# A transformer step on one core: the first two features between the modulation blocks, sums on GpSimd, and one context tile for four heads

## The reference

```python
mod = silu(c) @ w_mod + b_mod                       # 9 vectors of 1024
h = rmsnorm(x, ng[0]) * (1 + sc1) + sh1
x = x + g1 * 0.5 * (silu(h @ w_gate) * (h @ w_up)) @ w_down      # first FFN, 2816 features
h = rmsnorm(x, ng[1]) * (1 + sc2) + sh2
q, k, v, xr, xg = split(h @ w_in)
# latent tokens attend to latent keys and 128 cached ones, context tokens to context keys only
s = einsum(q, k) / 8                                # 4 heads, two maps each
p = softmax(s)
o = (p[map 0] - lam * p[map 1]) @ v                 # then rmsnorm of each head
# beside it: convolution, gates and a scan over time of xr, times gelu(xg)
x = x + g2 * concat(o, rg) @ w_out
x = x + g3 * 0.5 * swiglu(rmsnorm(x) ...)           # second FFN
```

## Time and profile before

| | us |
|---|---|
| median of 3 runs | 2238.14 |
| lowest, highest | 2234.83, 2238.75 |
| the profiled execution's own time | 2237.18 |
| its span | 2235.4 |
| mean granted TensorE clock | 0.993 |

### The profile page before, as it was taken

One profiled execution on the slowest core, in us unless ns is written; L12 is line 12 of the kernel. 1 busy time (PEld: TensorE's weight loads), 2 busy tenths in 40 slices (PEclk: granted clock), 3 DMA queues, 4 the chain that ended last, 5 costly groups with the idle time before them and its releaser, 6 DMA issues.

```text
span 2235.4 us, 34069 instructions
## 1 busy us (share of the span) xinstructions
PE 2161.9 (97%) x13144; PEld 2100.3 (94%) x13144; DVE 1537.1 (69%) x2543; ACT 825.0 (37%) x1503; POOL 67.6 (3%) x120
## 2 busy tenths in 40 slices
PE   5999999999999999999999999999999999999997
PEld 4989999999999999899988889899999999999996
DVE  6977777777878865766767874695555547756556
ACT  5632232234212133565257762453222323411122
POOL 0000000000000000000023130000000000000000
PEclk9999999999999999999999999999999999999999
DMA  7333323334534403001133211132121223521312
GB/s 294 134 106 121 120 96 136 105 123 141 179 127 157 145 19 150 30 29 48 38 84 110 55 41 38 61 112 89 59 84 63 75 72 113 179 94 59 114 31 85
DMA packets 86133, 219.03 MB, mean 98 GB/s; under 512 B 10624, under 2 KB 38144, under 8 KB 86016
## 3 DMA queue, kind: packets, MB, share of 16 engines
q1 hardware_dynamic: 82176, 208.52, 27.4%
q0 software_dynamic: 3840, 8.92, 1.8%
HBM read 172.56 MB, written 35.92 MB: 93 GB/s over the span
## 4 chain that ended last, share of the span: by engine, by line
PE 87%; DVE 6%; ACT 3%; DMA 2%; issue 1%; SPq 0%; DVEq 0%; POOL 0%; ACTq 0%
PE ps L818 15%; PE ps L819 15%; PE ps L820 15%; PE ps L893 9%; PE ps L895 9%; PE ps L894 9%; PE ps L1073 7%; PE ps L1204 2%; PE ps L1149 1%; PE ps L1055 1%; PE ps L1190 1%; PE ps L1157 1%; DMA sb_stage<-in_w_mod 1%; ACT sb_pr L1721 1%; DVE sb_nmx L2461 1%
## 5 line engine op out<-in xcount | busy, mean ns | idle before, releaser
L818 PE MATMUL ps<-sb_hH,sb_wH 128*128 128x384 f32 x1664 | 563.0, 338 | 9.5 <-DVE sb_hL L1915 4.7
L819 PE MATMUL ps<-sb_hL,sb_wH 128*128 128x384 f32 x1664 | 557.2, 335 | 0.0
L820 PE MATMUL ps<-sb_hH,sb_wL 128*128 128x384 f32 x1664 | 557.2, 335 | 0.0
L818 PEld LDWEIGHTS ps<-sb_hH,sb_wH 128*128 128x128 f32 x1664 | 313.1, 188 | 16.9 <-DVE sb_hL L1915 5.4
L819 PEld LDWEIGHTS ps<-sb_hL,sb_wH 128*128 128x128 f32 x1664 | 313.4, 188 | 1.2 <-issue 0.3
L820 PEld LDWEIGHTS ps<-sb_hH,sb_wL 128*128 128x128 f32 x1664 | 313.3, 188 | 0.0
L2225 DVE SCALAR_TENSOR_TENSOR sb_x<-ps,sb_mod,sb_x 128x384 f32<-128x384 f32 (+2 forms) x384 | 186.1, 514 | 172.2 <-PE ps L820 167.0
L893 PE MATMUL ps<-sb_hH,sb_wH 128*128 128x384 f32 x704 | 236.2, 336 | 5.1 <-DVE sb_tmp L2085 3.9
L894 PE MATMUL ps<-sb_hL,sb_wH 128*128 128x384 f32 x704 | 235.9, 335 | 0.0
L895 PE MATMUL ps<-sb_hH,sb_wL 128*128 128x384 f32 x704 | 235.7, 335 | 0.0
L1368 ACT ACTIVATE sb_wH<-sb_wide 128x512 fp32r<-128x512 f32 x176 | 110.9, 633 | 228.7 <-DVE sb_wide L1969 223.7
(11 more groups left out here) (259 smaller groups left out, 3799.7 us busy)
## 6 DMA issues: line engine op xcount, KB each, us to landing
sb_raw<-in_w_gate SPq DMA_DIRECT2D x56, 512.0 KB, 3.6
sb_raw<-in_w_up SPq DMA_DIRECT2D x56, 512.0 KB, 3.5
sb_raw<-in_w_mod SPq DMA_DIRECT2D x56, 512.0 KB, 3.6
hidden<-sb_tmp SPq DMA_DIRECT2D x132, 192.0 KB, 2.1
sb_hid_raw<-hidden SPq DMA_DIRECT2D x40, 576.0 KB, 6.4
sb_raw<-in_w_dn SPq DMA_DIRECT2D x80, 256.0 KB, 2.6
sb_stage<-in_w_mod SPq DMA_DIRECT2D x4, 2048.0 KB, 15.7
sb_raw<-in_w_in SPq DMA_DIRECT2D x16, 512.0 KB, 3.5
```

The lines of the kernel that those rows point to most:

```text
L818: pe.matmul(o, wH, xH, start=begin, stop=False)
L819: pe.matmul(o, wH, xL, start=False, stop=False)
L820: return pe.matmul(o, wL, xH, start=False, stop=end)
```

## The change

**Head.** The seven small tensors that nothing early needs are loaded behind the first two modulation blocks. The weights of feature 0 are loaded ahead of the third and fourth block, those of features 1 and 2 and chunks 1 and 2 of x behind them. PE computes the k-steps 0 to 3 of feature 0 between the modulation blocks, and afterwards parts of features 0 and 1 in turn (`early_part`), as k-tiles of h come. ScalarE's casts and VectorE's lows follow that order, one 128x512 half at a time (`early_one`). The series of the recurrence moves into the down projection (`series_step`). PE's modulation blocks use bank 2 in place of 6, and feature 2 the banks 2 and 7.

**GpSimd.** The seven additions of the squares of chunk 2 (`last_square`) and the four differences of each of the four pairs (`op_differences`, in both FFNs) move from VectorE to GpSimd.

**Attention.** The four context tiles become one: eight score matmuls in the value projection (behind piece 8), one maximum per map over four heads, eight exponentials, four differences, four transposes, one copy, four value matmuls. The loop runs over 32 latent tiles. `SPLIT_AT` is moved accordingly.

The diff, cut:

```diff
-TILES = NH * QT
-KEY_TILES = [1] + [9] * 8
-GROUP0 = [0] + [1 + 3 * t for t in range(9)]
-GROUPS = GROUP0[9]
+LT = LAT // P
+TILES = 1 + NH * LT
+KEY_TILES = LT + 1
+LAST_HEAD = 1 + (NH - 1) * LT
...
-SPLIT_AT = {4: (1, 1), 8: (2, 0), 10: (2, 1), 17: (3, 0), 20: (3, 1)}
+SPLIT_AT = {4: (1, 1), 7: (2, 0), 9: (2, 1), 14: (3, 0), 17: (3, 1)}
...
+        def early_bank(z, w, u):
+            return (2, 7)[u] if (z, w) == (0, 2) else 3 + u + 2 * (w % 2)
...
                 for w in range(EARLY - 1):
-                    load_one(z, 0, w + 2, (MAIN + w + 2) % FT)
-                    load_one(z, 1, w + 2, (MAIN + w + 2) % FT)
+                    if z:
+                        early_load(z, w + 2)
                     store(z, 0, 0, MAIN + w, w)
+                    if z == 0 and w + 4 <= EARLY:
+                        early_load(z, w + 4)
...
+            for b in MOD_FIRST[:2]:
+                stage_load(b)
+            for dst, name in LATER_SMALLS:
+                sp.dma_start(dst, a[name]).then_inc(gw_in, 16)
+            early_load(0, 0)
+            for b in MOD_FIRST[2:]:
+                stage_load(b)
+            early_load(0, 1)
+            early_load(0, 2)
             x_load(1)
-            load_one(0, 0, 1, MAIN + 1)
-            load_one(0, 1, 1, MAIN + 1)
             x_load(2)
+            early_load(0, 3)
             ffn_loads(0)
...
+            def last_square(k):
+                s, buf = nrm[0], sum_buf(0, 2)
+                n = square_at(0, 2, k)
+                pool.wait_ge(s["sq"], n + 1)
+                if k > 1:
+                    pool.wait_ge(s["acc"], added_at(0, 2, k - 1))
+                pool.tensor_tensor(buf, buf if k > 1 else tmp[:, (n - 1) % 2], tmp[:, n % 2], ALU.add).then_inc(s["acc"], 1)
+            def op_differences(z, p):
+                base = 16 * z + 4 * p
+                pool.wait_ge(front, base + 4)
+                pool.tensor_tensor(op_raw(T1, p), op_raw(T3, p), op_raw(B11, p), ALU.subtract).then_inc(front_pool, 1)
+                pool.tensor_tensor(op_raw(T3, p), op_raw(B22, p), op_raw(T3, p), ALU.subtract).then_inc(front_pool, 1)
+                pool.wait_ge(front_pool, base + 1)
+                pool.tensor_tensor(op_raw(T2, p), op_raw(B22, p), op_raw(T1, p), ALU.subtract).then_inc(front_pool, 1)
+                pool.wait_ge(front_pool, base + 3)
+                pool.tensor_tensor(op_raw(T4, p), op_raw(B21, p), op_raw(T2, p), ALU.subtract).then_inc(front_pool, 1)
+            for k in range(1, KT):
+                last_square(k)
+            for p in range(KT // 2):
+                op_differences(0, p)
...
+                op_differences(1, p)
...
             mod_products(0)
             spread(0, 0)
-            for n in range(1, PRE):
-                mod_products(n)
-            def first_chunk(z, u, n, w, between=None, index=0):
...
+                             {(2, 0, 2): (stats, 1), (2, 1, 0): (spread, 1), (2, 1, 5): (stats, 2), (3, 0, 3): (spread, 2)})
...
+            def early_part(n, u, ks):
+                first_chunk(0, u, n + 1, None, lambda k: pe.wait_ge(nrm[0]["h"], k + 1), n, ks)
+            early_part(0, 0, (0, 1))
+            mod_products(2)
+            early_part(0, 1, (0, 1))
+            for u in range(2):
+                early_part(0, u, (2, 3))
+            mod_products(3)
+            early_part(1, 0, range(4))
+            for k in (4, 5):
+                for u in range(2):
+                    early_part(0, u, (k,))
+            early_part(1, 1, range(4))
+            for k in (6, 7):
+                for u in range(2):
+                    early_part(0, u, (k,))
+            for u in range(2):
+                early_part(1, u, range(4, KT))
             ffn_pe(0)
...
+            def context_scores():
+                for hd in range(NH):
+                    for m in range(2):
+                        r = slice(m * DH, (m + 1) * DH)
+                        mm = pe.matmul(ps[:, 6 + m, hd * P:(hd + 1) * P], x[r, hd, 0:P], x[r, hd + NH, 0:P], start=True,
+                                       stop=True, tile_position=(m * DH, 0))
+                        if hd == NH - 1:
+                            mm.then_inc(s_ready, 1)
...
+                if g == 2:
+                    pe.wait_ge(gate_ev, 12 * RGT)
+                    pe.wait_ge(m_ev, 6 + 12 + QK * NC)
+                    context_scores()
...
+            def context_turn():
+                pe.wait_ge(pd_ready, 1)
+                pe.wait_ge(e_done, 2)
+                for hd in range(NH):
+                    m = pe.transpose(ps[:, 7, hd * P:(hd + 1) * P], ctx_probs(0, hd), ident[:])
+                m.then_inc(t_ready, 1)
...
+            v_last(15)
+            pe.wait_ge(v_ev, 15)
+            for u in range(1, TILES + 3):
                 if u < TILES:
                     scores(u)
-                if u == 0:
-                    v_last(15)
-                elif u == 1:
+                if u == 1:
+                    context_turn()
                     v_last(16)
                     v_last(17)
                 elif u == 2:
...
-            h_hi(0, 0, range(4))
-            early_cast(0, 0, 0)
+            h_hi(0, 0, (0,))
+            early_one(0, 0, A11)
+            h_hi(0, 0, (1,))
+            early_one(0, 0, A21)
+            h_hi(0, 0, (2, 3))
+            early_one(0, 0, A12)
+            early_one(0, 0, A22)
+            early_one(0, 1, A11)
             h_hi(0, 0, (4, 5))
-            early_cast(0, 1, 0)
+            early_one(0, 1, A21)
             h_hi(0, 0, (6, 7))
-            early_cast(0, 0, 1)
-            squares(0, 1, lambda c, k: (xin[c], 16))
-            early_cast(0, 1, 1)
+            early_one(0, 1, A12)
+            early_one(0, 1, A22)
+            def x_in(c, k):
+                return xin[c], 16
+            squares(0, 1, x_in, range(4))
+            early_cast(0, 0, 2)
+            squares(0, 1, x_in, range(4, KT))
+            early_cast(0, 1, 2)
             root_of(0, 1)
-            squares(0, 2, lambda c, k: (xin[c], 16))
+            silu_first(0, 0)
+            squares(0, 2, x_in, range(3))
             root_copy(0, 1)
-            early_cast(0, 0, 2)
+            squares(0, 2, x_in, range(3, KT))
+            silu_first(0, 1, early_bank(0, 1, 0))
+            early_cast(0, 0, 3)
+            early_cast(0, 1, 3)
+            load_root()
             root_of(0, 2)
-            silu_first(0, 0)
-            early_cast(0, 1, 2)
             root_copy(0, 2)
+            act.wait_ge(gw_in, N_LATER)
             ffn_act(0)
...
+            def context_exps():
+                for m in range(2):
+                    act.wait_ge(mx_ready, m + 1)
+                    for hd in range(NH):
+                        mm = act.activation(ctx_probs(m, hd), ps[:, 6 + m, hd * P:(hd + 1) * P], ACT.Exp,
+                                            bias=nmx_c[:, m, hd:hd + 1], accum_out=ctx_sums[:, hd, m:m + 1])
+                    mm.then_inc(e_done, 1)
...
                     qk_high(0, 1)
+                    context_exps()
                     act.wait_ge(acst, N_ACST)
                     act.activation(kcH[:], kc[:], ACT.Copy).then_inc(qk_hi, 1)
                 elif n == 12:
+                    act.wait_ge(small_in, 2)
+                    act.activation(lams[:, 2:4], lams[:, 0:2], ACT.Exp).then_inc(lam_e, 1)
...
-                dve.wait_ge(front, base + 4)
-                dve.tensor_tensor(op_raw(T1, p), op_raw(T3, p), op_raw(B11, p), ALU.subtract).then_inc(front, 1)
-                dve.tensor_tensor(op_raw(T3, p), op_raw(B22, p), op_raw(T3, p), ALU.subtract).then_inc(front, 1)
-                dve.wait_ge(front, base + 5)
-                dve.tensor_tensor(op_raw(T2, p), op_raw(B22, p), op_raw(T1, p), ALU.subtract).then_inc(front, 1)
-                dve.wait_ge(front, base + 7)
-                dve.tensor_tensor(op_raw(T4, p), op_raw(B21, p), op_raw(T2, p), ALU.subtract).then_inc(front, 1)
...
+            def low_at_tile(n, at):
+                return lambda k: early_one(0, n, at[k]) if k in at else None
+            apply(0, 0, low_at_tile(0, {1: A11, 2: A21}), range(0, 4))
             mod_add(2)
+            early_one(0, 0, A12)
+            early_one(0, 0, A22)
             mod_add(3)
             dve.wait_ge(mod_done, 4)
             scale_of(0, 4, KT)
+            apply(0, 0, low_at_tile(1, {4: A11, 6: A21}), range(4, KT))
+            early_one(0, 1, A12)
+            early_one(0, 1, A22)
+            for k in range(1, 4):
+                sum_square(0, 1, k)
+            early_low(0, 0, 2)
+            for k in range(4, KT):
+                sum_square(0, 1, k)
+            early_low(0, 1, 2)
+            inverse_of(0, 1)
+            hid_first(0, 0)
             shift_step(0)
-            early_low(0, 0, 0)
-            apply(0, 0, None, range(4, 6))
-            early_low(0, 1, 0)
-            apply(0, 0, None, range(6, KT))
-            early_low(0, 0, 1)
-            for k in range(1, KT):
```

(24 more changed lines are left out.)

265 lines of the change are left out of this document (149 added, 116 removed).

## The result

The changed kernel took 2243.58 us in the median (2241.61 to 2247.37, 11 executions), the kernel before beside it 2237.71. The ratio is 1.0028, 95% interval 1.0020 to 1.0037: slower by 0.28%, where 0.7% faster was forecast. Its profiled execution took 2246.73 us (span 2244.9), that of the kernel before 2237.18.

A forecast was written before the change was run, and what follows sets the result against it. PE, busy 2161.9 us, was taken as the bound, with waits in the head and before the Strassen products. Attention 13.9 - 1.4 and head 4.0 gave 16.5 off 2237.2, plus 1.0 for the median: 2221.5 us, range 2211 to 2231.

The forecast's parts named there:

- So 6.2 or 2.7; I take 4, for the whole head: Head: VectorE, relieved by GpSimd, reaches feature 5's product 6.2 or 2.7 us earlier; 4 taken, bounds 9.4 and -4.
- The squares of chunk 2 stand behind the first Silu on ScalarE: Head: these squares start from about 54 us, and GpSimd's seven sums of them last until 62.3.
- PE's wait of 4.5: Head, feature 2: PE asks for GpSimd's sum of squares at about 57.8 us and waits 4.5.
- the sum: Whole kernel: 13.9 - 1.4 + 4.0 = 16.5 us off 2237.2, giving 2220.7.
- 1 us ahead: Head up to feature 1: 6 us gained by the new order less 5 of new waits.
- 44.6 forecast: Head: time in us at which VectorE's last k-tile comes, where it came at 43.14.
- 13.9 us go: Attention, heads' boundaries: context-tile steps of 4.98, 4.95 and 4.00 us vanish, with PE keeping the latent steps' time.
- 12.5 forecast with its start: Attention: 13.9 us gained at heads' boundaries, with -1.4 for score, transpose and value work moved to its start.
- a step over 5.5: Attention: sign that the main part is wrong, if a boundary between heads still shows such a step, in us.
- 1 us of ScalarE: Attention: a split takes about 1 us and just fits ScalarE's slack of 0.97 in a latent step.
- The differences of the second FFN: Second FFN's front: sixteen differences on GpSimd costed at nothing, covered by six early features of 8 us each.
- The fourth rival: Both FFN fronts: GpSimd's differences take over 2.5 us, PE stands 17 us and more; 2240 to 2255, chance 0.05.

The follow-up runs named there:

- experiment 6: Kernel 5, but the 16 differences of the first FFN's front stay on GpSimd; 2229.32 us, 0.9967 of the kernel before.
- experiment 9: Kernel 5 plus 16 unneeded two-input subtractions on GpSimd in the first FFN's front; 2236.60 us, 1.0001 of the kernel before.
- experiment 2: The changed kernel with the differences of both FFNs' fronts back on VectorE, sums of squares still on GpSimd; 2240.52 us, 1.0016 of the kernel before.
- experiment 7: Kernel 5, but the seven sums of squares stay on GpSimd; 2228.58 us, 0.9962 of the kernel before.
- experiment 11: Kernel 5, but the hidden tile's stores again stand behind the weight loads, as in the changed kernel; 2232.24 us, 0.9971 of the kernel before.
- kernel 5: The changed kernel with sums of squares and both FFNs' differences back on VectorE, stores one place earlier, x's restore three score tiles later; 2227.96 us, 0.9945.
- experiment 8: Kernel 4 with SyncE's restore of x and first output-weight loads three score tiles later; 2222.25 us, 0.9932 of the kernel before.
- kernel 4: The kernel before with the change's attention part alone, head and both FFN fronts as before; 2231.59 us, 0.9975 of the kernel before.
- after: The changed kernel with the whole change, against the kernel before; 2243.58 us in the median, 1.0028, profiled execution 2246.73 us.
- kernel 3: The changed kernel with SyncE's restore of x and first output-weight loads three score tiles later; 2236.22 us, 0.9993 of the kernel before.
- kernels 1: The changed kernel with each store of a hidden tile one place earlier in SyncE's queue, first FFN's front; 2240.83 us, 1.0011 of the kernel before.
- experiment 10: Kernel 5 plus 16 unneeded one-input multiplications by 0.5 on GpSimd in the first FFN's front; 2230.69 us, 0.9969 of the kernel before.
- experiment 12: Kernel 4 with head 2's two splits one tile later, at tiles 8 and 10, restore unchanged; 2222.90 us, 0.9935 of the kernel before.

## Why the prediction was wrong

The direction was wrong: -16.5 us forecast, +5.9 between the medians and +9.5 between the profiled executions. The items below are in the terms of the latter.

- *"So 6.2 or 2.7; I take 4, for the whole head"* was the step that failed, by 14.4: the head costs 10.4. I put a price on GpSimd working at half speed beside VectorE and left VectorE at full speed beside GpSimd. The quoted sentence of the Trainium skill ("GPSIMD Engine Reference", section "Key points") does not say which of the two pays; here both do. Experiments 6 and 9 show VectorE's scalings and differences at 1.23 to 1.38 us beside GpSimd instead of 0.55 to 0.61, and experiment 2 its lows quick again without GpSimd; GpSimd's own go from 1.00 to as much as 1.46. Moving 8.8 us of work away made the gates 5.2 us later (experiment 6).
- *"The squares of chunk 2 stand behind the first Silu on ScalarE"* was right, but only PE's wait of 4.5 was priced (it was 4.97). The Silu of feature 1 stands behind the same squares, and VectorE stood idle 7.43 for it, at a cost of 2.4 us at the gates in experiment 7, just clear of the noise.
- The store's new place in SyncE's queue was not in the sum at all; by itself it costs 4.2 in VectorE's row and 5.8 in time (experiment 11). The line of the store stands unchanged in the diff; the loads around it had moved.
- *"1 us ahead"* for the head up to feature 1 came true in its rows: VectorE's last k-tile ends at 44.12 (43.37 + 0.75 in its rows above; 44.6 forecast), and the first two features are early. It is worth nothing, since in kernel 5 VectorE's work from feature 1 to 5 is all but unbroken and sets the end; the gates start no earlier than with the old head (experiments 5 and 8).
- *"13.9 us go"* was right as a mechanism. With the one collision removed, the attention gives 13.6 (experiment 8) against 12.5 forecast with its start. The collision took 7.05 (12.02 - 4.97), and my test for it ("a step over 5.5") found it. I had costed the splits as 1 us of ScalarE, and not what their stacking waits for. Of the 13.6 us, 7.8 went into the collision and the half clock behind it (532.0 in kernel 4 against 524.2 in 8) and 2.7 into the half clock at the attention's start (534.7 in after against 532.0 in 4), which leaves 3.1.
- *"The differences of the second FFN"* at nothing was right: kernel 3 has them on GpSimd and takes 795.9 us from the last k-tile on, the kernel before 795.8. The 2.2 us that after loses there go with a clock of 0.85, which kernel 5 has as well without GpSimd (experiment 2).
- The fourth rival, slower than before, had the right place and a wrong price: it let GpSimd be slow (2.5 to 3.3 us a difference, measured 1.21 to 1.46 beside VectorE) and again not VectorE.

In the terms of the sum: head -10.4 for +4.0, attention 3.1 for 12.5, and -2.2 behind the last k-tile for 0. How much of the head's 10.4 each of its causes takes isn't shown: the experiments take them out one at a time, and their effects overlap.

What stays open: why the attention's start has 10.2 us of half clock in the profiled executions of after and of kernels 5 and 11, 3.4 in that of 3 and 3.6 in that of before, and none in any other, though the instructions there are the same in all but before. In the traces of 5 and 8 the same waits of PE, 1.18 and 0.48 us, stand at this place, and only in 5 the clock falls. From gates to last k-tile it makes 3.5 us between these two. As open is the lower clock behind the last k-tile (0.84 to 0.85 in after and kernels 1, 5 and 11, 0.91 in 9 and 10, 1.00 in the others). No experiment was made on either, and one trace per kernel doesn't tell whether they belong to the kernel or to the execution.

## What to carry to other kernels

When work moves from VectorE to GpSimd, price what both do at the same time: here VectorE's instructions on two SBUF operands took GpSimd's pace while it ran, so what is relief is work that lies beside VectorE's idle time or beside its PSUM reads. It does no harm where VectorE isn't the limit: the second FFN's differences on GpSimd cost nothing. When one trace of each kernel is compared, look at the granted clock of each stretch before a difference is put down to the change. When the order of loads in a queue changes, walk each store or later entry of that queue and ask what the entry in front of it now waits for. Of two groups of transfers that both stand on a path, look at the issue times: five microseconds of distance were worth nine of time here.

## What the runs showed of the hardware

- VectorE's 128x384 subtraction of two SBUF tiles: 0.55 us alone, 1.23 to 1.38 beside GpSimd's two-input instruction (1.31, experiment 9), 0.54 to 0.86 beside a one-input one (1.27 to 1.36, experiment 10). Four 128x512 lows: 2.49 alone, 5.28 to 5.53 beside two-input ones (experiments 1, 2 and 6).
- GpSimd's 128x384 subtraction: 1.00 alone, 1.21 to 1.46 beside VectorE (after). A multiplication by a constant took about as long, 1.27 to 1.36, beside VectorE (experiment 10).
- VectorE's 128x384 product with one operand in PSUM took 0.54 to 0.56 in every case, beside GpSimd too (78.33 in after, 100.94 in experiment 9).
- Four transfers of 256 KB landed in 4.1 us at the median when issued 5 us behind four of 512 to 576 KB, and in 9.9 to 10.1 when issued at once with the last of them (experiment 12 against after and experiment 4).
